# Order of the work where the last gate block, the last projection pieces and the last attention item meet

## The reference

```
ar, ag, q, kc, vc, ks, vs, kw, vw, ng, ga, gb = split_proj(rms_norm(x), w_in)
y_lru = h * gelu(ag)                      # h: gated linear recurrence over ar
o_nsa = compressed + selected + window attention, gated by sigmoid(ng)
x = x + (sigmoid(ga) * (y_lru @ w_proj_a) + sigmoid(gb) * (o_nsa @ w_proj_b)) @ w_out
x = x + moe(rms_norm(x))                  # top 4 of 32 experts
```

## Time and profile before

| what | us |
|---|---|
| median of 3 runs | 1916.1 |
| lowest, highest | 1913.25, 1916.9 |
| the profiled execution's own time | 1916.32 |
| its span (first to last instruction) | 1914.7 |
| PE busy in the span | 1836.5 |
| DVE busy in the span | 1503.1 |
| ACT busy in the span | 1127.9 |

### The profile page before, as it was taken

How to read it: one execution, slowest core, us unless ns; L and a number is a source line. 1 busy time by engine, 2 the same in 40 slices (tenths; PEclk the granted TensorE clock), 3 DMA queues, 4 the chain that set the end, 5 groups by cost and what they waited for, 6 DMA issues and landing times.

```text
span 1914.7 us, 27423 instructions
## 1 busy us (share of the span) xinstructions
PE 1836.5 (96%) x9799; PEld 1505.8 (79%) x9799; DVE 1503.1 (79%) x1752; ACT 1127.9 (59%) x1124; POOL 243.0 (13%) x259
## 2 busy tenths in 40 slices
PE   5989899999999999999999999999999999999996
PEld 3888878787767677788888888888888888888885
DVE  7655775645355747999999999999999999999994
ACT  5235544433332435776776776776776776776772
POOL 0031000003312033111011011011011011011000
PEclk9999899999999999999999999999999999999998
DMA  5065111113419219999999999999999999999991
GB/s 223 6 212 180 59 61 60 48 67 110 133 40 299 69 59 362 386 374 370 394 372 373 390 374 373 388 375 370 391 376 371 391 374 372 391 374 368 398 362 46
DMA packets 76747, 514.23 MB, mean 269 GB/s; under 512 B 10744, under 2 KB 31296, under 8 KB 50800
## 3 DMA queue, kind: packets, MB, share of 16 engines
q1 hardware_dynamic: 58944, 454.19, 60.1%
q0 software_dynamic: 17584, 58.51, 11.4%
q10 hardware_dynamic: 144, 0.55, 0.1%
HBM read 490.36 MB, written 28.24 MB: 271 GB/s over the span
## 4 chain that ended last, share of the span: by engine, by line
PE 75%; issue 8%; DVE 7%; ACT 6%; DMA 3%; POOL 0%; ACTq 0%; DVEq 0%; SPq 0%; POOLq 0%
PE bank L1111 26%; PE bank L1129 14%; PE bank L666 7%; PE bank L718 5%; PE bank L579 3%; PE bank L607 3%; ACT qT_rounded L1492 3%; PE bank L960 2%; PE bank L1093 2%; PE bank L1087 1%; PE bank L935 1%; DVE slab L2212 1%; DVE slab L2215 1%; PE bank L1103 1%; PE bank L735 1%
## 5 line engine op out<-in xcount | busy, mean ns | idle before, releaser
L2165 DVE TENSOR_TENSOR ring_rounded<-ring,wide_rounded 128x2048 fp32r<-128x2048 f32 x192 | 431.4, 2288 | 50.7 <-ACT wide_rounded L1492 50.3
L1111 PE MATMUL bank<-ring_rounded,slab_rounded 128*128 128x512 f32 x1024 | 400.7, 391 | 0.0
L1492 ACT ACTIVATE wide_rounded<-ring 128x2048 fp32r<-128x2048 f32 x192 | 359.8, 1908 | 10.5 <-PE bank L1111 8.8
L1111 PE MATMUL bank<-xn_rounded,slab_rounded 128*128 128x512 f32 x1024 | 327.5, 391 | 0.0
L2165 DVE TENSOR_TENSOR ring_rounded<-ring,xn_rounded 128x2048 fp32r<-128x2048 f32 x128 | 292.9, 2288 | 16.6 <-ACT xn_rounded L1492 16.6
L1129 PE MATMUL bank<-wide_rounded,slab_rounded 128*128 128x512 f32 x768 | 259.0, 398 | 0.0
L1111 PE MATMUL bank<-wide_rounded,slab_rounded 128*128 128x512 f32 x768 | 247.3, 389 | 0.0
L1492 ACT ACTIVATE xn_rounded<-ring 128x2048 fp32r<-128x2048 f32 x128 | 244.0, 1907 | 0.0
L1111 PEld LDWEIGHTS bank<-ring_rounded,slab_rounded 128*128 128x128 f32 x1024 | 192.6, 188 | 41.5
L1111 PEld LDWEIGHTS bank<-xn_rounded,slab_rounded 128*128 128x128 f32 x1024 | 193.1, 189 | 40.4 <-issue 0.8
L2392 POOL DMA_INDIRECT out_y<-slab,small x32 | 85.0, 2656 | 1001.8 <-ACT slab L1567 1001.8
(11 more groups left out here) (443 smaller groups left out, 2994.4 us busy)
## 6 DMA issues: line engine op xcount, KB each, us to landing
ring<-in_w_exp SPq DMA_DIRECT2D x192, 2048.0 KB, 10.0
ring<-in_w_blk SPq DMA_DIRECT2D x40, 512.0 KB, 3.6
slab<-in_w_tok SPq DMA_DIRECT2D x4, 1304.0 KB, 15.2
ring<-in_w SPq DMA_DIRECT2D x8, 512.0 KB, 3.7
ring<-in_w_out SPq DMA_DIRECT2D x2, 2048.0 KB, 14.8
xn<-in_xT SPq DMA_DIRECT2D x4, 520.0 KB, 7.9
ring<-in_k_cmp SPq DMA_DIRECT2D x32, 64.0 KB, 3.2
ring<-in_k_cmp POOLq DMA_DIRECT2D x32, 64.0 KB, 3.1
```

The lines of the kernel that those rows point to most:

```text
L1111: r = mm(bank[:, c, :], a[:, 4 * h + k, :], w[:, k, :], start=False, stop=h == 1 and k == 3 and x == 2)
L1492: fn(WH[(2 * c + h) % 6], ring[:, half_of(c, h)], ACT.Copy).then_inc(S["wh_ready"], 1)
L2165: v.tensor_tensor(ring_r[:, half_of(c, h)], ring[:, half_of(c, h)], WHf[(2 * c + h) % 6], ALU.subtract)\
```

## The change

The table `want` gives item 24 no piece, items 25 to 28 five each, items 29 and 30 six each and item 31 none (before: five each for 25 to 30, the last two in 31). So PE finishes piece 95 in item 30.

`piece_of` changes what pieces 61 and 62 are: the last gate block is worked first for the feature blocks 0 to 3 of both output halves (pieces 60, 61), then for 4 to 7 of both (62, 63). ACT does `y_high` 0 to 3 in item 23 ahead of the two `gate_tanh` and of `block_high(34)`, with no wait for the gates; `y_high` 4 to 7 stay where they were.

At the end, DVE does `weights(31)` ahead of item 30's `merged_half`; ACT does `weights_high(0, 0)` in item 30, before `turned(31)`, and DVE `weights_low(0, 0)` behind `rows_low` 0 to 2 as before; PE does the four transposes before `values(31)`.

```diff
-        want = [(2, 2, 3, 0 if x == (3, 1, 0) else 5)[x[0]] for x in items]
+        want = [(2, 2, 3, (0, 5, 5, 5, 5, 6, 6, 0)[2 * x[2] + x[1] - 1])[x[0]] for x in items]
...
+        def piece_of(x):
+
+            if 4 * (2 * KD - 1) <= x < 8 * KD:
+                return 4 * KD - 2 + x % 2, (x - 8 * KD + 4) // 2
+            return divmod(x, 2)
...
-                j, part = divmod(x, 2)
+                j, part = piece_of(x)
...
-            values(NF - 1)
             pe.wait_ge(S["m_ready"], 2 * KD)
             for t in range(QT_N):
                 r = pe.transpose(bank[:, 7, t * P:(t + 1) * P], kvraw[:, t, VC:VC + P], ident[:, :])
             r.then_inc(S["vt_done"], 1)
+            values(NF - 1)
...
             def y_high(k):
                 act.wait_ge(S["y_ready"], k + 1)
-                act.wait_ge(S["gate_done"], 4 * KD)
+                if k == KD // 2:
+                    act.wait_ge(S["gate_done"], 4 * KD)
...
+                if i == YH_AT:
+                    for k in range(KD // 2):
+                        y_high(k)
                 for j in range(upto[i] // 2, upto[i + 1] // 2):
                     if j < 4 * KD:
                         gate_tanh(j)
...
-                if i in (YH_AT, YH_AT + 1):
-                    for k in range(KD // 2):
-                        y_high(KD // 2 * (i - YH_AT) + k)
+                if i == YH_AT + 1:
+                    for k in range(KD // 2, KD):
+                        y_high(k)
                 if i == NF - 2:
                     for s in range(3):
                         rows_high(s)
+                    weights_high(0, 0)
...
-            for b in range(4):
+            for b in range(1, 4):
                 weights_high(0, b)
...
+                if i == NF - 2:
+                    weights(i + 1)
                 for j in range(max(upto[i] // 2, 4 * KD), upto[i + 1] // 2):
                     merged_half(j - 4 * KD)
-                if i + 1 < NF:
+                if i < NF - 2:
                     weights(i + 1)
...
                     for s in range(3):
                         rows_low(s)
+                    weights_low(0, 0)
...
-            for b in range(4):
+            for b in range(1, 4):
                 weights_low(0, b)
```

## The result

The changed kernel is slower. Its median is 1921.72 us (1913.84 to 1926.48) beside 1916.02 us (1909.94 to 1919.02) for the kernel before on the same chip: ratio 1.0029, interval 1.0017 to 1.0042. That is 5.6 us, by the interval 3.3 to 8.0, where 3.0 were forecast: in the direction forecast, nearly twice the size, and at the upper edge of the forecast's range. A second timing, 8 executions beside 31 of the kernel before, gave 1.0039 (1.0026 to 1.0053). The profiled execution took 1923.55 us; its span is 1921.9.

The account below looks back on a forecast made before the run. PE, busy 1836.5 of 1914.7 us, was taken as the bound, so only its waits count. Rounding Y in two parts 1.6 plus piece 94 and the last item 1.4 gave 3.0 us: 1919.1 us, range 1915.3 to 1921.7.

Parts of the forecast that it names:

- Part 1's delay without the clock: Rounding Y in two parts, item 23: later `block_high(34)` delays DVE's low parts and piece 65; costs 1.6 us.
- Part 2's wait: Item 30: PE stands still 2.7 us before piece 94, waiting for `merged_half(13)` to free bank 7.
- The 4.2 us before piece 65: PE's wait before piece 65 was to grow from 2.2 to over 4 us.
- the vanished wait for the first weight block: Before hidden step 0: PE's 2.3 us wait for the low part of the first compression weight disappears.
- the short one for `rows_low(3)`: Before hidden step 3: PE waits shortly for `rows_low(3)`, which ends at 458.8 against PE's possible 458.2.
- the idle DVE before `block_low(34)`: Item 23: DVE stands idle before `block_low(34)`, which waits for `block_high(34)`, ending near 371.4, 1.6 us later.
- part 2 without a drop: Piece 94 to hidden step 3, clock staying up: gains at the end pay for piece 94's wait; -0.1 us.
- the term of the clock: Low clock behind PE's waits: no extra at piece 65, a new 1.45 us at piece 94, 1.45 saved at step 0.
- the clock does what it did before: Condition on the 1.6 us at piece 65: low clock there unchanged; bounds +0.7 to +3.2.
- The rival "slower": Wait over 4 us before piece 65 keeps clock low over following pieces: 3.2 there, sum 4.6, 1920.7 us; chance 0.23.
- At piece 94 the drop: Low clock of 3.3 us behind the 2.7 us wait, costing 1.45; brings the end-of-stage changes to 1.4 us.
- the gain of the drop that vanishes at step 0: Hidden step 0: without the wait before it, its low clock goes too, winning 1.45 us.

Follow-up runs that it names:

- part 2 only: Kernel before plus new table of pieces, `weights(31)` before item 30's merges, weight block 0 split in item 30, transposes before `values(31)`; Y's rounding as before; ratio 1.0002.
- waits filled: Changed kernel with matmuls nobody reads put before pieces 65 (34) and 94 (22); ratio 1.0007 against the kernel before.
- part 1 only: Kernel before plus pieces 61 and 62 exchanged and `y_high` 0 to 3 ahead of the tanhs and `block_high(34)`; ratio 1.0007 against the kernel before.
- merge first: Changed kernel with `merged_half(13)` ahead of `weights(31)` on DVE in item 30; 0.0 us (-1.7 to 1.9) against the kernel before.
- before, third: Kernel before, unaltered, third profile: a single execution of 1915.45 us, no ratio.
- the eight experiments: In order: part 1 only, part 2 only, low parts first, merge first, both mended, waits filled, both mended plus 16 filler matmuls before piece 65 (ratio 0.9985), part 2 mended.
- low parts first: Changed kernel with `y_low` 0 to 3 ahead of `block_low(34)` on DVE in item 23; 1.3 us (-0.6 to 3.4) slower than the kernel before.
- both mended: Changed kernel with `y_low` 0 to 3 ahead of `block_low(34)` and `merged_half(13)` ahead of `weights(31)` on DVE; ratio 0.9991 against the kernel before.
- part 2 mended: Kernel before plus the changes of part 2 only, with `merged_half(13)` ahead of `weights(31)`; median 1914.49 us, ratio 0.9989 against the kernel before.

## Why the prediction was right and wrong

**Right: the waits and the direction.** Part 1's delay without the clock was put at 1.6 us and measured 1.5. Part 2's wait was put at 2.7 us and measured 2.7, because DVE does `weights(31)` before `merged_half(13)`; moving that one instruction removes it. The 4.2 us before piece 65, the vanished wait for the first weight block, the short one for `rows_low(3)` and the idle DVE before `block_low(34)` are all as written.

**Slightly off: part 2 without a drop.** It was put at -0.1. With the clock up at piece 94, stage 2 is 65.51 and 65.48 us (part 2 only, waits filled) against 64.98 before: +0.5. Pieces 94 and 95 take 3.15 and 3.14 us in those two rather than 2.88, turn(31) 1.04 in both rather than 0.87.

**Wrong: the term of the clock.** The step that failed is the count and length of the drops, at both ends of the comparison. What one of 3.4 us costs was sized rightly: 1.45 us forecast, 1.3 to 1.7 measured.

- In the changed kernel the wait before piece 65 was priced on the condition that "the clock does what it did before". Every profile with that wait of 4.2 us, five of five (changed three times, part 1 only, merge first), has 6.8 us of low clock there, where the kernel before has 3.4 twice and none once. Stage 1 takes 2.2 us more than in the first profile of the kernel before, against the forecast 1.6. The rival "slower" had this mechanism, with 3.2 for it, and a chance of 0.23. Its mechanism is what happened. Its 3.2 was too much, and its sum of 4.6 lies within the interval of the timed 5.6 (3.3 to 8.0).
- At piece 94 the drop came. Stage 2 is 66.95 - 64.98 = 1.97 us longer against the forecast 1.4: 0.5 is the term above, and the drop itself cost 66.95 - 65.48 = 1.5, as forecast. But in one profile of three it lasted 6.8 us and stage 2 took 68.16.
- The kernel before was read in one profile, which had both of its drops. A third profile has neither, and there the two stages take 2.6 us less. The prediction took the gain of the drop that vanishes at step 0 as whole, 1.45 us, but in one profile of three it was not there to win.

The means of three profiles each are 92.4 us for the two stages before and 97.6 in the changed kernel, +5.2. Against the timed 5.6 (3.3 to 8.0) and 7.5 (5.0 to 10.2) that is the right size. They come apart with the two sets of stages that have no drop: 90.67 us (before, third) and 94.03 (waits filled). The waits alone are thus 3.4, 1.5 in stage 1 and 1.8 in stage 2; the low clock adds 92.4 - 90.7 = 1.8 on average before and 97.6 - 94.0 = 3.6 after. In the same terms the forecast had 1.6 + 1.35 for the waits (1.35 is its -0.1 without the 1.45 us that it counted as won at step 0) and two drops of 1.45 in either kernel. The table carries the reading further, with one profile for each kernel: taken against 92.4, "both" gives +2.7, +1.0, +2.3, +0.6, -2.2, +1.6, -3.7 and -2.9 for the eight experiments, and the times say 1.3, 0.4, 1.3, 0.0, -1.7, 1.3, -2.9 and -2.1. Each lies within 1.5 us, in the same order; the profiles overstate every loss and every gain, by 0.3 to 1.4 us.

The Trainium skill ("TensorE: Matmul & The Clock Gate", HAM oscillation) warns only of idle gaps longer than ours of 2.2 to 2.7 us. The traces go against it: waits of 2.2 and 2.3 us drew 3.4 us of low clock in two of the three profiles of the kernel before. The same page of the Trainium skill, in its part "What's actually happening", says of a kernel's start that the number of matmuls at the low clock differs from run to run of one kernel, by the phase at which the start falls. The traces show such a difference in mid-kernel, 3.4 and 0 us behind the same wait; that a phase is its cause, no run here shows. The prediction did not use that remark, which speaks against counting the drops of one profile as certain.

**What stays open.** Why the parts do not add. With one long wait taken away the timed loss is 1.3 us or less, whichever it is; with both it is 5.6 or 7.5. The granted clock of the timed executions says of what kind the difference is. Its mean is 0.9848 in 35 executions of the kernel before, 0.9843 with part 1 alone and 0.9861 with part 2 alone (11 each), but 0.9831 and 0.9826 in the changed kernel (14 and 8), where the kernel before had 0.9852 in the 31 executions beside the latter. As an estimate, each 0.001 over a span of 1916 us is 1.9 us of full speed lost: part 1 alone loses 1 us more than before and part 2 alone 2.5 us less, while both together lose 3.3 to 5.0 us more. So what the two parts lose beyond their waits shows as low clock; where in the span it falls, these figures do not say. Piece 94's drop was there in all three profiles of the changed kernel and with the low parts first, but not in the one profile of part 2 alone. Whether the position of piece 94, later or earlier by a few us as part 1 decides, sets how often the drop falls there, would take many profiles of each; no run here shows it.

## What to carry to other kernels

An operand made ready earlier is worth nothing while its consumer's queue stands at another instruction: here four instructions of DVE moved at the first place and one at the second turned the change from 5.6 us slower into a tie, and with the wait filled into 2.9 us faster. Where PE waits for some 2 us or more in a kernel like this one, price the wait twice, once for itself and once for the low clock behind it (1.3 to 1.7 us for 3.4 us of it), and ask whether more than one profile shows the drop before you count on losing or winning it. For a change of a few us, compare stages over several profiles, and not spans.

## What the runs showed of the hardware

- Over 365 to 800 us, every stretch of low clock in the 14 profiles was 3.4 or 6.8 us long. One of 3.4 us cost 1.3 to 1.7 us.
- A wait of 4.2 us was followed by 6.8 us of it in five profiles of five. Of the 14 waits of 2.2 to 2.7 us at piece 65, piece 94 and step 0, nine were followed by 3.4 us of it, one by 6.8, and four by none (two in the third profile of before, piece 94 in part 2 only, piece 65 in part 2 mended). A wait of 1.9 us before piece 65 was followed by 3.4 us in both profiles that have it (low parts first, both mended).
- Matmuls whose results nobody reads, issued into a wait, kept the granted clock at 1.00, and gave 2.0 and 1.5 us at the two places.
- Over the whole span the low clock adds up to 60.1, 60.4 and 53.6 us in the three profiles of before and to 69.7, 69.6 and 63.3 in those of the changed kernel: 9.5 us more on average. As an estimate, at half speed that is up to 4.7 of the 6.5 us between the mean spans (1914.4 and 1920.9).
